# Twelve ring slots in place of ten, and half of the v tiles in 1 MB transfers

## What is computed

```python
def peer_ffn(...):
    q = (xb @ w_query).reshape(-1, PEER_HEADS, 2, PEER_QHALF)
    s = einsum('thpd,pkd->thpk', q, sub_keys)          # 2 x 128 sub-keys
    ...                                                # top 16 of 128, twice; top 16 of the 256 sums
    g = softmax(top_s)
    act = gelu(einsum('thkd,td->thk', u_tab[eidx], xb))
    return einsum('thk,thkd->td', g * act, v_tab[eidx])
```

## Time and profile before

| | us |
|---|---|
| median of 3 runs (lowest, highest) | 1614.41 (1612.65, 1618.49) |
| the profiled execution's own time | 1615.82 |
| its span in the profile | 1613.8 |
| PE busy | 1582.1 (98%) |
| DVE busy | 1101.5 (68%) |
| POOL busy | 494.1 (31%) |

### The profile page before, as it was taken

The page is one execution under the profiler, slowest core; times in us unless marked ns, Lnnn a source line. Parts: engine busy times, 40 slices in busy tenths (PEclk is TensorE's granted clock), DMA queues, the critical chain, the costliest instruction groups (busy, mean ns, idle before and its releaser), DMA issues.

```text
span 1613.8 us, 30119 instructions
## 1 busy us (share of the span) xinstructions
PE 1582.1 (98%) x12128; PEld 1506.9 (93%) x12128; DVE 1101.5 (68%) x2478; ACT 209.5 (13%) x604; POOL 494.1 (31%) x423
## 2 busy tenths in 40 slices
PE   9999999999899999999999999999999999999997
PEld 7688899999899999998898888999999999999997
DVE  3373379998899998545537425999879989944441
ACT  2251221111011000000003312111211100000000
POOL 0000033335444456533300001333534435533310
PEclk9999999999999999999999999999999999999999
DMA  6304489999999999999984446999999999999991
GB/s 245 131 16 147 137 304 389 384 394 406 409 408 409 401 409 408 409 409 409 409 326 155 144 149 227 339 397 386 396 409 408 408 405 408 408 410 408 409 378 60
DMA packets 149979, 534.94 MB, mean 331 GB/s; under 512 B 17617, under 2 KB 20434, under 8 KB 149842
## 3 DMA queue, kind: packets, MB, share of 16 engines
q1 hardware_dynamic: 89938, 314.90, 50.7%
q0 software_dynamic: 59904, 218.13, 34.5%
HBM read 531.92 MB, written 1.05 MB: 330 GB/s over the span
## 4 chain that ended last, share of the span: by engine, by line
PE 79%; DVE 10%; DMA 8%; issue 3%; ACT 0%; DVEq 0%; SPq 0%; ACTq 0%; POOLq 0%
PE ps L267 37%; PE ps L1159 30%; DMA raw<-in_v_rows 6%; PE ps L1122 4%; DVE big L1322 3%; PE ps L728 2%; PE ps L279 2%; DMA big<-in_u_rows,big 2%; DVE big L1272 1%; PE ps L1501 1%; PE ps L738 1%; DVE big L1268 1%; PE ps L1433 1%; DVE big L1298 1%; DVE big L1300 1%
## 5 line engine op out<-in xcount | busy, mean ns | idle before, releaser
L267 PE MATMUL ps<-big,raw 128*128 128x160 f32 (+2 forms) x5104 | 798.5, 318 | 2.5 <-ACT big L1225 2.5
L267 PEld LDWEIGHTS ps<-big,raw 128*128 128x128 f32 x5104 | 751.5, 191 | 35.6 <-issue 3.1
L1159 PE MATMUL ps<-big,raw 128*128 128x160 f32 x4096 | 579.1, 301 | 6.5 <-DVE big L1154 2.3
L1159 PEld LDWEIGHTS ps<-big,raw 128*128 128x128 f32 x4096 | 559.6, 190 | 15.7 <-DMA raw<-in_v_rows 12.7
L1185 POOL DMA_INDIRECT big<-in_u_rows,big x208 | 250.3, 1203 | 733.4 <-DVE big L1308 376.5
L1339 DVE SCALAR_TENSOR_TENSOR big<-big 128x1024 f32<-128x1024 f32 x201 | 258.0, 1284 | 191.3 <-PE ps L1159 107.7
L1185 POOL DMA_INDIRECT big<-in_v_rows,big x208 | 240.5, 1156 | 320.6 <-DVE big L1339 255.1
L1322 DVE CUSTOM_DVE_ANT_0 big<-big 128x1024 f32<-128x1024 f32 x208 | 244.4, 1222 | 22.4 <-DMA big<-in_u_rows,big 19.8
L1225 ACT ACTIVATE big<-ps 128x160 f32<-128x160 f32 x256 | 77.4, 303 | 512.7 <-PE ps L267 474.0
L374 ACT ACTIVATE big<-h 128x272 f32<-128x272 f32 (+1 forms) x32 | 12.7, 419 | 645.8 <-DVE h L1414 597.3
L1268 DVE MAX8 big<-big 128x8 f32<-128x128 f32 (+1 forms) x99 | 33.5, 339 | 88.3 <-ACT big L1194 76.3
(11 more groups left out here) (173 smaller groups left out, 762.7 us busy)
## 6 DMA issues: line engine op xcount, KB each, us to landing
raw<-in_u SPq DMA_DIRECT2D x256, 512.0 KB
raw<-in_v_rows SPq DMA_DIRECT2D x256, 512.0 KB
raw<-in_query SPq DMA_DIRECT2D x32, 512.0 KB
raw<-in_lru_w SPq DMA_DIRECT2D x24, 512.0 KB
raw<-in_mla_down SPq DMA_DIRECT2D x17, 512.0 KB
raw<-in_mla_out SPq DMA_DIRECT2D x8, 512.0 KB
big<-in_u_rows,big POOLq DMA_INDIRECT x208
big<-in_v_rows,big POOLq DMA_INDIRECT x208
```

Source lines behind the costliest of these rows:

```text
L267: mm = pe.matmul(out, w[:, c * P:(c + 1) * P], x[:, c, :], start=(c == 0), stop=(c == DC - 1))
L1159: return pe.matmul(accumulator(c), w, act_w[:, i, :], start=start, stop=False, skip_group_check=True)
```

## The change

The ring has 12 slots in place of 10. The descriptor scratch is 8,192 bytes in each partition in place of 16,384, and the two extra slots (8,192 bytes in each partition) lie in what that frees. The v tiles come from a second copy of the table, `v`, in which partition p of a pair of tiles has its two rows of 4 KB side by side. By turns such a pair comes in one transfer of 1 MB, which takes 8 KB in a row for each partition and fills two neighbouring slots, and the next pair comes in two transfers of 512 KB. A pair's transfer waits until both of its slots are free, and counts once for both tiles. The gathers still read `v_rows`. Tile g lies in slot (g + 1) % 12, so that a pair never wraps.

```diff
-SLOTS = 10
+SLOTS = 12
...
+        for count, _ in transfers:
+            k = self.slot(self.total)
+            assert k + count <= SLOTS
+            used[k] = used[k] + 16
+            self.sem_of = self.sem_of + [self.landed[k]] * count
+            self.count = self.count + [used[k]] * count
+            self.total = self.total + count
...
+    def slot(self, g):
+        return (g + 1) % SLOTS
...
     def fetch(self, sp, first, last):
-        for g in range(first, min(last, len(self.tiles))):
-            if g >= SLOTS:
-                sp.wait_ge(self.done, 2 * (g - SLOTS + 1))
-            sp.dma_start(self.mem.raw[:, g % SLOTS, :], self.tiles[g]).then_inc(self.landed[g % SLOTS], 16)
+        g = 0
+        for count, tiles in self.transfers:
+            if first <= g < last:
+                k = self.slot(g)
+                if g + count > SLOTS:
+                    sp.wait_ge(self.done, 2 * (g + count - SLOTS))
+                sp.dma_start(self.mem.raw[:, k:k + count, :], tiles).then_inc(self.landed[k], 16)
+            g = g + count
...
+        v = []
+        for k in range(NK // 2):
+            two = d["v"][n][k]
+            v = v + ([(1, two[:, 0:1, :]), (1, two[:, 1:2, :])] if k % 2 else [(2, two)])
...
+    def by_two(tiles):
+        tiles = tiles.reshape(layers, -1, 2, P, D).transpose(0, 1, 3, 2, 4)
+        return np.ascontiguousarray(tiles)
...
+        "v": by_two(a["peer_v"]),
...
-    nc = bacc.Bacc("TRN2", target_bir_lowering=False, num_devices=1)
+    nc = bacc.Bacc("TRN2", target_bir_lowering=False, num_devices=1, dynamic_dma_scratch_size=8192)
```

More of the change, by code:

```diff
@@ L215, with __init__, wait_landed @@
 class Tiles:
-    def __init__(self, ctx, mem, tiles):
-        self.mem, self.tiles = mem, tiles
+    def __init__(self, ctx, mem, transfers):
+        self.mem, self.transfers = mem, transfers
         self.landed = [ctx.sem(f"landed{k}") for k in range(SLOTS)]
         self.done = ctx.sem("tiles_done")
-    def fetch(self, sp, first, last):
-        for g in range(first, min(last, len(self.tiles))):
-            if g >= SLOTS:
-                sp.wait_ge(self.done, 2 * (g - SLOTS + 1))
-            sp.dma_start(self.mem.raw[:, g % SLOTS, :], self.tiles[g]).then_inc(self.landed[g % SLOTS], 16)
+        self.sem_of, self.count, self.total, used = [], [], 0, [0] * SLOTS
+        for count, _ in transfers:
[7 more added lines that the diff above has]
+        return (g + 1) % SLOTS
+    def wait_landed(self, pe, g):
+        pe.wait_ge(self.sem_of[g], self.count[g])
+    def fetch(self, sp, first, last):
+        g = 0
[6 more added lines that the diff above has]
+            g = g + count
 class Stream:
@@ L252, in wait_landed @@
     def wait_landed(self, pe, n):
-        g = self.base + n
-        pe.wait_ge(self.mem.tiles.landed[g % SLOTS], 16 * (g // SLOTS + 1))
+        self.mem.tiles.wait_landed(pe, self.base + n)
     def tile(self, n):
-        return self.mem.raw[:, (self.base + n) % SLOTS, :]
+        return self.mem.raw[:, self.mem.tiles.slot(self.base + n), :]
     def multiply_raw(self, pe, n, out, x, scaled=None):
@@ L1553, in tiles_in_order, with single @@
 def tiles_in_order(d):
+    def single(tile):
+        return 1, tile.unsqueeze(1)
     def layer(n):
[L1556 to L1561, removed]
+        v = []
+        for k in range(NK // 2):
+            two = d["v"][n][k]
+            v = v + ([(1, two[:, 0:1, :]), (1, two[:, 1:2, :])] if k % 2 else [(2, two)])
+        return [single(d["query"][n][k]) for k in range(2 * PH)] + [single(d["u"][n][k]) for k in range(NK)] + v
+    mixed = [[single(d["mla_down"][k]) for k in range(MLA_TILES - DC)] + [single(d["mla_out"][k]) for k in range(DC)],
+             [single(d["lru_w"][k]) for k in range(LRU_TILES)]]
     return mixed[0] + layer(0) + mixed[1] + layer(1)
@@ L1655, in lay_out @@
     lru_in = a["lru_w_in"][0]
-    u = a["peer_u"].reshape(layers, NK, NK, DC, P).transpose(0, 1, 4, 3, 2)
+    u = a["peer_u"].reshape(layers, NK, NK, DC, P).transpose(0, 1, 4, 3, 2).reshape(layers, NK, P, D)
+    def by_two(tiles):
+        tiles = tiles.reshape(layers, -1, 2, P, D).transpose(0, 1, 3, 2, 4)
+        return np.ascontiguousarray(tiles)
     return {
@@ L1667, in lay_out @@
         "keys": np.ascontiguousarray(a["peer_sub_keys"].transpose(0, 3, 1, 2)),
-        "u": np.ascontiguousarray(u).reshape(layers, NK, P, D),
+        "u": np.ascontiguousarray(u),
+        "v": by_two(a["peer_v"]),
         **{f"u_rows{n}": np.ascontiguousarray(a["peer_u"][n]) for n in range(layers)},
```

## The result

The changed kernel takes 1625.43 us in the median of 5 runs (1624.90 to 1625.66), the kernel before 1613.97 us (5 runs). The ratio is 1.0067, 95% interval 1.0056 to 1.0078: 11.5 us slower. Forecast were 1610.0 us and "the same" (0.74); slower had 0.13, and the range ended at 1622. What happened is rival A, which had 0.27 and the time 1622.

What follows compares the result with a forecast made beforehand. TensorE, busy 98%, was taken as the bound, starved for tiles in layer 0's v stage by full DMA engines. Terms -4.4 - 0.6 + 0.6 = -4.4 us took the median of 1614.4 to 1610.0 us; range 1605 to 1622.

Steps and rivals of the forecast that it cites:

- rival A: Layer 0's v stage: an 8 KB packet gets a 4 KB packet's turn, gathered rows come late; +8, 1622 us, chance 0.27.
- part 1: Layer 0's starved v stage: two more slots put TensorE two tiles of 2.176 us further, -4.4 us.
- the last fold waits for nothing: Sign that the forecast is right: in layer 0's v stage TensorE has no wait before the last fold.
- the clock: Rival A's term: a 20 us stand of TensorE before layer 0's last fold lowers its clock, 2 us lost.
- Part 2: v tile pairs with 8 KB in a row have half the packets: -0.6 us taken, at most -1.5 us.
- Part 3: Pairs' transfers wait for both slots and land later: +0.6 us taken in layer 0's starved stretch, 0 in layer 1.
- Part 4: Half the descriptor scratch for POOL's gathers: 0 taken, up to +2 us if POOL had to wait for space.
- The cap: Layer 0's last fold needs all gathered rows, so only 6.7 us can be won before it waits for rows.

Runs made afterwards that it cites:

- e2_pairs_of_4k_packets: The change, but each partition of a 1 MB pair gets its 8 KB as two 4 KB packets from rows 512 KB apart: 1610.43 us, 0.9981 of before.
- e4_all_pairs: The change, but with all v tiles in pairs of 8 KB packets: 1624.39 us, 1.0060 of the kernel before.
- e1_slots_alone: Kernel before with twelve slots and half the scratch, every v tile in its own 512 KB transfer of 4 KB packets: 1609.62 us, 0.9968 of before.
- e10_one_pair: Twelve slots and half the scratch, all tiles single except layer 0's v tiles 96 and 97, one 8 KB-packet pair: 1615.01 us, 0.9998 of before.
- e6: The change, but in layer 0 no next-stage tile is issued until VectorE has used the last gathered row: 1618.73 us, 1.0014 of before.
- e8: Twelve slots, one pair in four in 8 KB packets, other tiles single, layer 0's next-stage tiles held back: 1618.43 us, 1.0018 of before.

## Why the prediction was wrong

**The step that failed** is in part 1: "While both queues are backlogged, tiles and rows go on at one each in 2.56 us whatever TensorE does." That is so for equal packets, and the trace of before had only those. With 8 KB packets the turns stay even by count, and the bytes go 4 to 3 (14.05 to 10.66 MB). On this step rested the -4.4 us for a kernel with pairs, and the forecast put the wait in front of the last fold at nothing ("the last fold waits for nothing"). Measured were a wait of 21.6 us, a fold 6.5 us late, and 4.0 us for the lower clock behind it.

The prediction had this written down as rival A. The rows of the trace of before fit turns by packets and turns by bytes alike, so they gave no ground for 0.45 on the forecast against 0.27 on the rival.

The Trainium skill ("DMA: Bandwidth & Descriptors", "Queues, rings and completion order") has each engine go round its queues packet by packet. The traces agree on the turns, with 2933 to 2928 packets. The page gives a packet about 9 to 17 descriptors, while what the profile counts as a packet here is one run of 4 or 8 KB. How many such runs make a turn is not shown; the runs show that the shares go by their number, and not by whole transfers (`e2_pairs_of_4k_packets`, 12.40 to 12.07 MB).

**Rival A's own working** came out nearly to the number: TensorE at the last fold without starving (817.6 us foreseen, 837.63 - 21.6 = 816.0 measured), the fold 6.0 us late (6.5 measured). A part of that is luck: it summed only bytes, and the last seven rows went at VectorE's 1.42 us each and not at the DMA's 1.28, 1.0 us more. Mis-sized was the clock: 2 us foreseen, 4.0 measured (1.9 in the fold, 2.1 in the tiles). It had been read off a wait of 4.9 us, with 7 us at 1.2 GHz, some 4 of them with work. Here the clock had fallen and stayed low while TensorE still stood, so that all of the next 7.4 us of work, from 837.6 to 845 us, ran at 0.50. With 4 in place of 2 rival A would have said 1624.

**Part by part.** Part 1, two slots: -4.4 foreseen, -4.9 measured, when alone. Part 2, fewer packets: 413 GB/s in place of 409 between 720 and 780 us, which as an estimate is 1.0% of some 195 us, 1.9 us of transfer time. The upper bound was 1.5 us, and the term was taken as 0.6. 825 packets of 8 KB (5865 less the 5040 under 8 KB) are 6.8 of the 24.8 MB, 27%; if the whole gain is theirs, they go some 3.7% faster. By the same working `e4_all_pairs`, with 58% of the bytes in such packets and 1.6% more moved, gives 2.8%. It did not help, as the last rows came late all the same. By the Trainium skill's 3 cycles per packet ("DMA: Bandwidth & Descriptors", "Why small descriptors are slow") the estimate was 1.1% for the pairs' bytes. Both traces give more than that by this working. Part 3, pairs: 0.6 foreseen; with 4 KB packets 0.1 us in the traces and 0.8 us in the medians, neither clear of nothing; layer 1 unchanged, as foreseen. Part 4, scratch: 0 and 0. The cap, that only 6.7 us could be won before the fold waits for rows, fits what was measured: with the fold 5.15 us earlier (`e1_slots_alone`) TensorE did not wait for rows, with TensorE there 7.6 us earlier (`e10_one_pair`) it did.

**Left open:** when the clock falls behind a short wait (1.1 us in one trace, not 1.4 us in the other), and whether two backlogged queues would reach 2 to 1. Not tried was a split that favours the gathers: v tiles in packets of less than 4 KB should give it if turns go by packets. Larger packets for the gathers are not to be had, since a row of the table has 4 KB.

## What to carry to other kernels

Two queues that were both backlogged shared the DMA engines here by packets: the one with packets of 8 KB took bytes from the one with 4 KB, so a larger packet was a priority and not only an efficiency. Before giving a stream priority, find the last thing that the other one must deliver, and its margin (6.7 us here): past it, the waits only change their place. And put a price on a wait of TensorE that includes the matmuls behind it at the lower clock (3.2 to 4.6 us here); 35 waits of 0.4 us kept the clock, a single one of 3.1 us did not.

## What the runs showed beyond that

Waits of 0.4 us, 35 times, left the granted clock at 1.00; one wait of 3.1 us in front of the fold (`e10_one_pair`) doubled the time of the fold behind it, 3.56 us in place of 1.69, and cost 3.6 us in all, more than the wait. Of TensorE's waits for tiles with 4 KB packets none, up to 2.0 us each, is followed by a lower clock: from 630 to 860 us it was granted at 1.00 in `e1_slots_alone` and in `e2_pairs_of_4k_packets`. And VectorE's chained adds, 1.28 to 1.30 us long, repeat each 1.42 us in the chains of the change, e6 and e8, which is slower than the 1.28 us in which 512 KB land at 409 GB/s: once the tiles no longer took their share, the gathers were bound by VectorE.
